# Cross attentions head by head between weight slabs, and a combine of the experts by a 0/1 matrix with y in two parts

## The reference

```python
def memory_cross_attention(h, mem_n, wq, wkv, wo):        # 4 heads of 256, 256 memory tokens
    q = (h @ wq) ... ; k, v = split_cols(mem_n @ wkv, (D, D))
    p = jax.nn.softmax(einsum('blhd,bmhd->bhlm', q, k) * (XA_HD ** -0.5), axis=-1)
    return einsum('bhlm,bmhd->blhd', p, v) @ wo

def moe_swiglu(h, router_w, w_gate, w_up, w_down):        # top 2 of 8, hidden width 3584
    gates = ...                                           # (256, 8), softmax over the two chosen
    for e in range(N_EXPERTS):
        out = out + gates[:, e:e + 1] * swiglu(t, w_gate[e], w_up[e], w_down[e])
```

## Time and profile before

| | |
|---|---|
| profiled execution, its own time | 1726.68 us |
| its span | 1724.9 us |
| TensorE matmul busy | 1673.4 us, 97% |
| VectorE busy | 1297.6 us, 75% |
| ScalarE busy | 1039.2 us, 60% |
| mean granted clock of TensorE | 0.985 |
| moved from HBM | 459.72 MB, 267 GB/s over the span |

### The profile page before, as it was taken

How to read it: one execution, slowest core, us unless ns; L and a number is a source line. 1 busy time by engine, 2 the same in 40 slices (tenths; PEclk the granted TensorE clock), 3 DMA queues, 4 the chain that set the end, 5 groups by cost and what they waited for, 6 DMA issues and landing times.

```text
span 1724.9 us, 23270 instructions
## 1 busy us (share of the span) xinstructions
PE 1673.4 (97%) x8662; PEld 1419.5 (82%) x8662; DVE 1297.6 (75%) x1120; ACT 1039.2 (60%) x935; POOL 21.0 (1%) x32
## 2 busy tenths in 40 slices
PE   6999999999999999699999999999999999999997
PEld 5997879999887797688888888888788788788785
DVE  6783645555467764698888888888888988988886
ACT  5341435444356544577677677677677677677674
POOL 1000000000000100000000000000000000000000
PEclk9996999999999999899999999999999999999999
DMA  8651525655654445499899899999879999999992
GB/s 314 200 190 50 176 93 171 196 174 192 195 172 137 132 147 198 150 369 370 323 365 372 315 380 359 322 370 372 324 277 365 325 366 349 340 375 342 346 371 120
DMA packets 222435, 461.44 MB, mean 268 GB/s; under 512 B 7314, under 2 KB 52580, under 8 KB 222388
## 3 DMA queue, kind: packets, MB, share of 16 engines
q1 hardware_dynamic: 221696, 459.53, 75.0%
q0 software_dynamic: 528, 1.22, 0.2%
q10 hardware_dynamic: 164, 0.04, 0.0%
HBM read 459.72 MB, written 1.05 MB: 267 GB/s over the span
## 4 chain that ended last, share of the span: by engine, by line
issue 60%; PE 35%; DVE 3%; ACT 1%; DMA 0%; POOL 0%; ACTq 0%; DVEq 0%; POOLq 0%
PE ps L1518 14%; PE ps L1504 8%; PE ps L1743 4%; PE ps L1666 3%; PE ps L1627 1%; PE ps L1594 1%; PE ps L1613 1%; PE ps L1584 1%; DVE w_lo L368 1%; PE ps L1692 0%; ACT w_hi L364 0%; ACT a_hi L542 0%; DMA rows<-in_ev_conv_w 0%; DVE a_lo L879 0%; DVE u L1035 0%
## 5 line engine op out<-in xcount | busy, mean ns | idle before, releaser
L368 DVE TENSOR_TENSOR w_lo<-raw,w_hi 128x2048 fp32r<-128x2048 f32 x431 | 981.8, 2290 | 248.2 <-ACT w_hi L364 246.8
L364 ACT ACTIVATE w_hi<-raw 128x2048 fp32r<-128x2048 f32 x431 | 826.8, 1919 | 364.5 <-PE ps L1893 138.1
L1893 PE MATMUL ps<-w_hi,e_hi 128*128 128x512 f32 x896 | 354.2, 395 | 3.1 <-DVE e_lo L1369 3.1
L1893 PE MATMUL ps<-w_hi,e_lo 128*128 128x512 f32 x896 | 349.6, 390 | 0.0
L1893 PE MATMUL ps<-w_lo,e_hi 128*128 128x512 f32 x896 | 349.0, 389 | 0.0
L1893 PEld LDWEIGHTS ps<-w_hi,e_hi 128*128 128x128 f32 x896 | 168.3, 188 | 36.5 <-issue 3.3
L1893 PEld LDWEIGHTS ps<-w_hi,e_lo 128*128 128x128 f32 x896 | 168.2, 188 | 35.8
L1893 PEld LDWEIGHTS ps<-w_lo,e_hi 128*128 128x128 f32 x896 | 168.4, 188 | 33.6
L1915 PE MATMUL ps<-w_hi,at_hi 128*128 128x512 f32 x448 | 175.0, 391 | 1.9 <-DVE at_lo L1381 1.9
L1915 PE MATMUL ps<-w_hi,at_lo 128*128 128x512 f32 x448 | 174.4, 389 | 0.0
L1915 PE MATMUL ps<-w_lo,at_hi 128*128 128x512 f32 x448 | 174.3, 389 | 0.0
(11 more groups left out here) (294 smaller groups left out, 1816.0 us busy)
## 6 DMA issues: line engine op xcount, KB each, us to landing
raw<-in_moe_w_up SPq DMA_DIRECT2D x112, 1024.0 KB, 6.9
raw<-in_moe_w_gate SPq DMA_DIRECT2D x110, 1024.0 KB, 7.0
raw<-in_moe_w_down SPq DMA_DIRECT2D x110, 1024.0 KB, 6.1
raw<-in_xa_wkv SPq DMA_DIRECT2D x16, 1024.0 KB, 5.1
raw<-in_ev_w_in SPq DMA_DIRECT2D x14, 1024.0 KB, 8.7
raw<-in_od_w_in SPq DMA_DIRECT2D x12, 1024.0 KB, 5.0
raw<-in_ffd_w_gate SPq DMA_DIRECT2D x11, 1024.0 KB, 5.4
raw<-in_ffd_w_up SPq DMA_DIRECT2D x11, 1024.0 KB, 5.3
```

Of the source, the lines that this page charges most:

```text
L364: nc.scalar.activation(w_hi[:, n % CUT, :], at_, ACT.Copy).then_inc(hi_cut, 1)
L368: nc.vector.tensor_tensor(w_lo[:, n % CUT, :], place(n, r, behind)[0], w_hi[:, n % CUT, :].bitcast(F32), ALU.subtract).then_inc(lo_cut, 1)
L1893: mm = T.matmul(ps[:, bank, :], s, m, start=(h == 0 and k == 0 and j == 0), stop=(h == 1 and k == 3 and j == 2))
```

## The change

Both `cross`: the heads go one after the other between slabs. Output slabs are taken by K half (K half 0 of both column halves first), since K half 0 needs heads 0 and 1 only. Scores use banks 4 and 5 in turn, probabilities bank 6, values bank 7.

The combine: `pack` itself is transposed, `spread` is fp32r (0 and 1), y is split into `y_hi` (ScalarE) and `y_lo` (VectorE), the gate is multiplied in the addition to X, and `pgate` goes.

```diff
-            slabs[f"o{i}"] = t_all(kpn(xa_wo[i]))
+            slabs[f"o{i}"] = [t_slab(kpn(xa_wo[i]), 512 * b)[h] for h in range(2) for b in range(2)]
 # TensorE, cross
+                q_slab(0)
+                q_slab(1)
+                scores(0)
+                q_slab(2)
+                scores(1)
+                turn_p(0)
+                q_slab(3)
+                values(0)
+                scores(2)
+                turn_p(1)
+                scores(3)
+                values(1)
+                o_slab(0, 0, {2: lambda: turn_p(2)})
+                values(2)
+                turn_p(3)
+                o_slab(1, 0, {2: lambda: values(3)})
+                o_slab(0, 1, {})
+                o_slab(1, 1, {2: lambda: turn_x(0)} if i == 1 else {})
 # waits: scores(h>=2) on exps(h-2); turn_p(h) on shares(h) and turned(h-1);
 #        values(h) on turned(h) and head_lo(h-1); each k of an o_slab on its head's head_lo
 # ScalarE, cross; cut(n) is cut_hi of slab FIRST[q]+n+AHEAD
+                cut(0); cut(1); cut(2); exps(0); cut(3); turned(0); exps(1); head_hi(0); turned(1)
+                exps(2); head_hi(1); exps(3); cut(4); turned(2); head_hi(2); turned(3); cut(5)
+                head_hi(3); cut(6)
+                if i == 0:
+                    cut(7)
 # VectorE, cross (one call a line there)
+                cut(0); q_got(0); cut(1); q_got(1); top(0); cut(2); shares(0); q_got(2); top(1); cut(3)
+                shares(1); q_got(3); head_lo(0); top(2); top(3); shares(2); head_lo(1); shares(3)
+                cut(4); head_lo(2); cut(5); head_lo(3); cut(6)
+                dve.wait_ge(slab_used, FIRST[f"o{i}"] + 3)
+                x_event(0, f"o{i}")()
                 if i == 0:
+                    cut(7)
+                    dve.wait_ge(slab_used, FIRST[f"o{i}"] + 4)
+                    x_event(1, f"o{i}")()
 # experts
-                    V.tensor_tensor(X[:, t, :], ps[...], X[:, t, :],
-                                    ALU.add).then_inc(x_half if t == 0 else combined, 1)
+                    V.scalar_tensor_tensor(out=X[:, t, :], in0=ps[...],
+                                           scalar=gate16[:, t, bass.ds(col, 1)], in1=X[:, t, :], op0=ALU.mult,
+                                           op1=ALU.add).then_inc(x_half if t == 0 else combined, 1)
+            def y_up(q):                      # ScalarE, between the cuts of G0+1 and G0+2
+                act.wait_ge(slab_used, G0 + PASS + PASS * q)
+                nc.scalar.activation(y_hi[:, :], ps[:, 2:4, :]..., ACT.Copy).then_inc(y_top, 1)
             def v_y(q):
-                dve.wait_ge(slab_used, G0 + PASS + PASS * q)
-                V.tensor_copy(y[:, :], ps[:, 2:4, :]...).then_inc(y_sb, 1)
+                dve.wait_ge(y_top, q + 1)
+                V.tensor_tensor(y_lo[:, :], ps[:, 2:4, :]..., y_hi[:, :].bitcast(F32),
+                                ALU.subtract).then_inc(y_sb, 1)
-                    add_pass(q)
+                    add_pass(q, column(q - 1))          # column: a register load from a table
-                        mm = T.matmul(ps[:, b0 + o, :], spread[:, t * P:(t + 1) * P], y[:, 512 * o:512 * o + 512],
-                                      start=True, stop=True)
+                        for yv in (y_hi, y_lo):
+                            mm = T.matmul(ps[:, b0 + o, :], spread[:, t * P:(t + 1) * P],
+                                          yv[:, 512 * o:512 * o + 512], start=yv is y_hi, stop=yv is y_lo)
-                pe.wait_ge(pg_rdy, q + 1)
-                    mm = T.transpose(ps[:, 5, t * P:(t + 1) * P], pgate[:, t, :], ident)
+                    mm = T.transpose(ps[:, 5, t * P:(t + 1) * P], pack[:, t, :], ident)
```

More of the change, by code:

```diff
@@ L150, in trunk_kernel @@
         ta = sb("ta", [P, 2048])
+        with ExitStack() as s:
+            sb("tb_front", [P, D], F32, s)
+            y_lo = sb("y_lo", [P, D], F32R, s)
         tb = sb("tb", [P, 2048])
@@ L196, in trunk_kernel @@
             pack = sb("pack", [P, 2, BLK], F32, s)
-            pgate = sb("pgate", [P, 2, BLK], F32, s)
-            spread = sb("spread", [P, 2 * P], F32, s)
-            y = sb("y", [P, D], F32, s)
+            spread = sb("spread", [P, 2 * P], F32R, s)
+            y_hi = sb("y_hi", [P, D], F32R, s)
+            sb("e_spare", [P, 2 * BLK], F32, s)
             ones = sb("ones", [P, P], F32, s)
@@ L820, in a_next @@
                 pack_hi(q)
-                for n in range(1, 6):
+                cut_hi(act, G0 + 1, 7 * q, behind)
+                y_up(q - 1)
+                for n in range(2, 6):
                     cut_hi(act, G0 + n, 7 * q, behind)
@@ L841, in _ @@
                 a_pass(q, [(1, NB, True)])
+            y_up(n_pass - 1)
             n_fin = 2 + 2 * [n for n in NORMS if n != "ret"].index("fin")
@@ L1052, in cross, with q_got, top, shares @@
                 turn_lo(name, a_hi, a_lo)
[L1054 to L1058, removed]
+                def q_got(k):
+                    dve.wait_ge(slab_used, FIRST[f"q{i}"] + k + 1)
+                    freed(V.tensor_copy(xq[:, 2 * k:2 * k + 2, :], acc(f"q{i}", k, 1)), 1)
+                def top(h):
                     dve.wait_ge(xs_ps, XH * i + h + 1)
-                    link(V.tensor_reduce(mx[:, 2 * h:2 * h + 2], pair(4 + h), AX.X, ALU.max))
+                    link(V.tensor_reduce(mx[:, 2 * h:2 * h + 2], pair(4 + h % 2), AX.X, ALU.max))
                     V.tensor_scalar(nmx[:, 2 * h:2 * h + 2], mx[:, 2 * h:2 * h + 2], -1.0 / 16.0, None,
                                     ALU.mult).then_inc(xs_mx, 1)
-                for h in range(XH):
+                def shares(h):
                     dve.wait_ge(xs_exp, 2 * (XH * i + h + 1))
@@ L1069, in cross, with head_lo, cut @@
                     ins.then_inc(xs_n, 1)
-                for h in range(XH):
+                def head_lo(h):
                     dve.wait_ge(xs_hi, XH * i + h + 1)
-                    V.tensor_tensor(a_lo[:, 2 * h:2 * h + 2, :], pair(4 + h), a_hi[:, 2 * h:2 * h + 2, :].bitcast(F32),
+                    V.tensor_tensor(a_lo[:, 2 * h:2 * h + 2, :], pair(7), a_hi[:, 2 * h:2 * h + 2, :].bitcast(F32),
                                     ALU.subtract).then_inc(xs_lo, 1)
+                def cut(n):
+                    cut_lo(dve, FIRST[f"q{i}"] + n + AHEAD)
+                cut(0)
+                q_got(0)
+                cut(1)
+                q_got(1)
+                top(0)
+                cut(2)
+                shares(0)
+                q_got(2)
+                top(1)
+                cut(3)
+                shares(1)
+                q_got(3)
+                head_lo(0)
+                top(2)
+                top(3)
+                shares(2)
+                head_lo(1)
+                shares(3)
+                cut(4)
+                head_lo(2)
+                cut(5)
+                head_lo(3)
+                cut(6)
+                dve.wait_ge(slab_used, FIRST[f"o{i}"] + 3)
+                x_event(0, f"o{i}")()
                 if i == 0:
-                    stage("o0", 4, {1: x_event(0, "o0"), 3: x_event(1, "o0")})
+                    cut(7)
+                    dve.wait_ge(slab_used, FIRST[f"o{i}"] + 4)
+                    x_event(1, f"o{i}")()
             cross(0, xa_q0, xa_v0)
@@ L1270, in _ @@
             cross(1, xa_q1, xa_v1)
-            stage("o1", 3, {1: x_event(0, "o1"), 2: lambda: turn_lo("moe", a_hi, a_lo, tiles=range(4))})
+            turn_lo("moe", a_hi, a_lo, tiles=range(4))
             dve.wait_ge(slab_used, FIRST["o1"] + 4)
@@ L1388, in add_pass @@
                     dve.wait_ge(c_ps, 2 * done + t + 1)
-                    V.tensor_tensor(X[:, t, :], ps[:, b0:b0 + 2, :].rearrange("p a n -> p (a n)"), X[:, t, :],
-                                    ALU.add).then_inc(x_half if t == 0 else combined, 1)
[L1392 to L1398, removed]
+                    V.scalar_tensor_tensor(out=X[:, t, :], in0=ps[:, b0:b0 + 2, :].rearrange("p a n -> p (a n)"),
+                                           scalar=gate16[:, t, bass.ds(col, 1)], in1=X[:, t, :], op0=ALU.mult,
+                                           op1=ALU.add).then_inc(x_half if t == 0 else combined, 1)
             cut_lo(dve, G0 + 2)
             pack_lo(0)
-            pack_gates(0)
             for n in range(3, 6):
@@ L1459, in _ @@
             v_y(n_pass - 1)
-            add_pass(n_pass)
+            add_pass(n_pass, column(n_pass - 1))
             dve.wait_ge(in_fin, 16)
@@ L1484, in room, with slab_t, gemm_t @@
                     pe.wait_ge(acc_free, upto - 4)
-            def gemm_t(name, blocks, hi, lo, base=None, before_last=None):
+            def slab_t(n, bank, h, hi, lo, before_k=None):
+                slab_ready(n)
+                wh, wl = (shaped(w[:, n % CUT, :], 4) for w in (w_hi, w_lo))
+                for k in range(4):
+                    if before_k is not None:
+                        before_k(k)
+                    for t in range(2):
```

(27 more changed lines are left out.)

59 lines of the change are left out of this document (42 added, 17 removed).

## The result

The changed kernel takes 1713.06 us (median of 4 runs, 1712.12 to 1713.6) against 1727.51 us before in the same comparison: ratio 0.9917, 95% interval 0.99 to 0.9934. So it is 14.45 us faster by these medians, 0.8%; the forecast was 14.5 us less, or 1713.7 us from a median of three runs of the kernel before. The profiled execution of the changed kernel spans 1710.3 us (1724.9 before), at a mean granted clock of 0.984. TensorE's matmuls are busy for 1660.0 us in place of 1673.4.

What follows compares the result with a forecast made beforehand. TensorE, busy 97% of the span, was taken as the bound. Combine -11.3, first cross attention -5.3 and second +2.1 sum to -14.5 us, giving 1713.7 us against the 1728.24 median; range 1708 to 1719, meant to hold 8 in 10.

Steps and rivals of the forecast that it cites:

- three parts: Terms of the sum: combine -11.3 us, first cross attention -5.3, second cross attention +2.1.
- The combine's price: Expert passes: eight fp32r matmuls take 1.82 us where four f32 took 3.43; 1.61 saved in seven passes, 11.3 us.
- The wait two slabs later: Slab G0+2 after each combine: VectorE's cut has 0.1 us margin behind y_up; 0.05 a pass booked, 0.35 us for seven.
- VectorE behind the combine: Expert passes: VectorE's cut of G0+6 still ends in time, 0.35 us early; register load taken as 0.
- Rival C: Register load before the combine's additions makes VectorE the bound; at 3 us each 1732 us, slower; chance 0.02.
- The end: Exposed last combine: y_up and hand-over added, second half ready sooner; 0.3 us less, between -1 and +1.
- First attention: First cross attention: head by head order between slabs saves 6.0 us less 0.7 for switches, -5.3 us, no clock fall.
- The walk: First cross attention stepped through slab by slab from measured rows: all waits met, end at 263.5 instead of 269.54.
- returns from attention to slabs: First cross attention: some ten slower slab restarts after transposes, at 0.08 us each, 0.7 us; between 0 and 1.6.
- Rival B: Head by head order stalls in both attentions, each giving back 5 us; sum -9.2, 1719 us; chance 0.15.
- Second attention: Second cross attention: late G0 load through three queues stops TensorE 5.1 us, then half clock; +2.1 us instead of -5.3.
- rival A: Second cross attention: the G0 load is no obstacle, so -5.3 us there too; sum -21.9, 1706.3 us; chance 0.12.

Runs made afterwards that it cites:

- y_late: Changed kernel with y_up and v_y one slab later, behind the cuts of G0+2 instead of before them: 1714.91 us, ratio 0.9932.
- g0_early: Changed kernel with the first expert's four opening loads sent before SP's wait for the values, held_u after it: 1708.07 us, ratio 0.989.
- g0_first: Changed kernel with SP's wait kept, but the first expert's opening loads sent before the two held_u slabs: 1705.59 us, ratio 0.9877.
- cross_only: Kernel before with only the new order of both cross attentions: 1724.87 us, ratio 0.9988.
- warm: both plus ten f32 matmuls of the unit matrix, result unused, behind the first gather: 1706.2 us, ratio 0.9879.
- both: Changed kernel with the edits of g0_first and y_late together: 1706.46 us, ratio 0.9879 to the kernel before.
- combine_only: Kernel before with only the new combine: 1717.21 us, ratio 0.9941.

## Why the prediction was right, point by point

The mechanisms of all three parts were forecast rightly, and each sum is within 1 us of its stage. That the total fits to 0.1 us is partly luck, as said below.

- **The combine's price was right**: 1.82 us by the distance between slab matmuls, 1.82 measured; 1.61 saved seven times, 11.3 us. The wait two slabs later was mis-sized: booked 0.05 a pass, it came to (11.3 - 10.4) / 7 = 0.12. VectorE's cut of G0+2 ends at 839.05 for a use at 839.13, about the margin forecast. What the sum left out is the weight load ahead of that matmul: before the change it starts 0.23 us ahead of its matmul (842.96 and 843.19), now only 0.03 ahead (839.10), after a wait of 0.23 us for the cut. y_late takes 0.1 a pass of it away by that order alone.
- **VectorE behind the combine** kept its cover: forecast a margin of 0.35 us at G0+6, measured 0.23. The register load before the additions costs nothing visible: the first starts 0.60 us after `e_mul` does (846.32 and 846.92), as the additions did before (850.27 and 850.87). Rival C is out.
- **The end**: booked -0.3, measured -0.1.
- **First attention**: booked -5.3, measured -5.90. The walk gave 6.0 (60.73 us from q0 to the end; 60.87 measured), and the 0.7 for returns from attention to slabs was too much: half a slab lasts 2.75 to 2.77 us in place of 2.72 behind such a return, some 0.1 us in all. The clock stays at 1.00 there. Rival B is out.
- **Second attention**: the mechanism is as forecast, in the order of the three queues. G0 landed 10.7 us after the release (10.5 booked), TensorE waited 5.2 us (5.1), the clock cost 1.65 (1.7 to 1.9), and the sum is +1.19 (+2.1). The difference is again the returns to slabs, 0.6, and the clock. g0_early and g0_first remove the late load, which is what rival A supposed, and save 6.9 us, where that rival had 7.4.
- **Not forecast**: +1.35 us in the first expert slab, by the clock, and -0.74 us before the first attention, which no part of the change explains. The attentions gave 1.5 us more than booked, the passes and the end 0.7 less. These errors cancel: 14.5 us were forecast and 14.6 of span measured. The 0.6 us between 1713.7 and 1713.06 comes from the two medians of the kernel before (1728.24 and 1727.51).
- With the load in the way TensorE resumed at half clock (0.50 at 681), and g0_early and g0_first, without the wait, save its 1.65 us too. The Trainium skill's rule on bursts parted by a DMA wait (page "TensorE: Matmul & The Clock Gate", section "HAM oscillation — how this bites in real kernels") describes this; the trace agrees, for a wait of 5.2 us whose chain starts with a load.

## What to carry to other kernels

When work is pulled forward on one engine, ask what still hangs on its old end on the others: here the loads of the next stage waited for the last value product, and what made it cost 5 us was the order in three queues behind them, two less urgent slabs first, the cut before the residual. Send what is used first, and leave no urgent small operation behind a cut that waits for a load. A part that changes a busy TensorE by fewer matmul passes is priced well by the pitch of its neighbours.

## What the runs showed of the hardware that was not expected

At two short waits the granted clock came out differently from profile to profile, though TensorE had waited about as long. Before the last down slabs TensorE waits 1.86 to 1.87 us in all ten profiles; from the last transposes to the end four of them take 123.3 to 123.5 us (before, after, cross_only, g0_early), warm 124.3, and five 125.0 to 126.0. In g0_first the first matmul behind that wait reads

```profile
1680.91 0.68 PE L2020 MATMUL ps<-w_hi,at_hi 128*128 128x512 f32 x1 [1.86 <-DVE at_lo L1454]
```

(both has the same 0.68 us) where the others have 0.49, and the slabs behind it run at half clock for a time; in combine_only the fall comes later. The first expert slab ran at full clock in three of ten profiles (before, g0_first, warm: 36.5 to 36.7 us from router to transposes) and lost 1.2 to 2.0 us in the other seven; the waits before it were 3.1 and 2.9 us in before and g0_first (0.3 in warm), and 2.6 to 3.4 in the slow ones. In each of the nine other profiles the two places together cost 0.9 to 3.7 us more than in the kernel before, as much as most single edits here.

The stage before the first attention, which no edit touches, ends anywhere from 200.86 to 204.47 us in the ten profiles. And one and the same kernel varies: fifteen runs of the kernel before on one chip took 1723.87 to 1729.45 us, the five fastest at a mean granted clock of 0.987, the three slowest at 0.983. What decides whether the clock falls at a short wait is not shown. So a difference of 2 to 3 us between two profiles says nothing about an edit unless it lies in the stage that was edited.
